# When heads leave PSUM, and what scores and the output projection wait for, in the last two layers of a two-block transformer kernel

## Chip, cores and metric

One core of a Trainium2 chip runs the whole program. The metric is the time of one execution on the device in microseconds (us), lower is better. All matrix products are in float32. The engines are named as in the profile: PE is TensorE (PEld its weight loads), DVE is VectorE, ACT is ScalarE, POOL is GpSimd, SP is the queue that issues most DMAs.

## What is computed

The input is x, 256 tokens of 1024 channels. A first block (convolution mixer, mixture of 16 experts, attention and long convolution, experts again) runs up to about 1560 us. The change doesn't touch it. A second block of two layers follows:

```python
for l in range(DEPTH):                                     # 2 layers
    x = x + 0.5 * swiglu(rms_norm(x, ffn1_norm[l]), ...)   # D_FF = 2816
    h = rms_norm(x, mix_norm[l])
    z = h @ w_in[l]
    qa, ka, va, qs, ks, vs, zg = split(z)
    qa, ka = rms_norm per head (8 heads of 64)             # neighbourhood attention
    qs, ks = rms_norm per head (8 query, 2 key heads)      # sliding window attention
    o_na = softmax(qa @ ka.T / 8 + bias_na) @ va
    o_sw = softmax_with_sink(qs @ ks.T / 8 + bias_sw) @ vs
    g = sigmoid(zg + b_gate[l])                            # 2 x 1024 gates per token
    merged = g[0] * (o_na @ w_branch_na[l]) + g[1] * (o_sw @ w_branch_sw[l])
    x = x + merged @ w_out[l]
    x = x + 0.5 * swiglu(rms_norm(x, ffn2_norm[l]), ...)
```

## The kernel before

**Layout.** Channels lie on the 128 partitions and tokens on the free axis, so a 1024-channel tensor is 8 blocks (KB = 8) of 128 x 256. Weights come through one stream of 1 MB chunks into a ring of 12 slots, in the order in which PE uses them. SP issues each chunk when PE has freed the slot that it goes to (L672). A chunk of w_in holds 256 output columns: the projection of one chunk (`project`, L1317) is two halves of 8 matmuls into one PSUM bank, 32 matmul records of 256 columns in the trace, since a float32 matmul leaves two records.

**Order of work.** Each engine has a hand-written program. Every engine has one counter, each of its instructions that matter raises it, and the others wait for a value of it. A wait for a value that the same engine has already waited for or passed is left out (`Engine.wait_ge`, L195), so a wait is emitted only where it asks for something later than all waits before it on that counter. DVE's counter follows its program order: waiting for a late DVE instruction covers all earlier ones.

**Heads** (PE L1379 to L1420, ACT L1863 to L1874, DVE L2469 to L2507). The seven groups of heads come in the order qa 0, qa 1, ka 0, ka 1, qs 0, qs 1 (two blocks each, 512 columns) and ks 0 (256 columns). They alternate between PSUM banks 5 and 4. For group i:

- PE projects it, and after that makes the sums of squares of group i-1 (`norm_heads` of PE, L1371: one matmul of 512 columns into bank 6). That matmul waits for ACT's square of group i-1 (L1373) and, where a group precedes it, for ACT's root of group i-2 (L1375).
- DVE's `copy_heads` (L2469, L2480) takes it out of its bank, multiplied by the token scale.
- ACT squares the copy (L1870), waits for the sums and takes their root (L1539).
- DVE's `norm_heads` (L2482) inverts the root (L1944, a reciprocal) and scales the group (L2488).
- The loop of DVE (L2490) runs `norm_heads` of group i-1 first and `copy_heads` of group i second.

Between the heads' end and the scores stand the values: vs (32 records of 128 columns), va of the first 128 tokens, the sums of ks, va of the last 128 tokens (L1405 to L1420). DVE takes them out, then copies the two halves of ks crosswise into KSX (L2506, L2507, the signal `ks_swapped`). KSX is read only by sliding-window scores.

**Attention** (PE L1433 to L1501). Eight pairs of heads: m = 0 to 3 are neighbourhood pairs, 4 to 7 sliding-window pairs. For each pair PE makes `scores(m)` into banks 0 and 1, projections of gates as filling, transposes of the probabilities (`turned`) and `values`. Before its scores PE waits for `ks_swapped` (L1441), and from the second pair on for DVE to have read the scores of the pair before.

**Branches and output** (PE L1477 to L1518, DVE L2549 to L2562). Eight calls of `branch(p, n)`, p = 0 to 3 and n = 0, 1, fill bank 2(p mod 2) + n with 16 records each. DVE multiplies each by its gates (`gated`, L2555) and adds the two of one p into two blocks of `merged` (L2557). Then the output projection: four chunks c into banks 0 to 3, each two halves of 8 matmuls over k, where matmul k reads block k of `merged`. PE waits for the last `merged` ahead of all of them (L1510).

Of the kernel before, what the change touches and what calls it, by code (L numbers as in the profile page):

```python
# [14 lines left out]
KB = D // P  # L15
# [528 lines left out]
def head_of(M, what, c):  # L544

    y = M.late
    return y.KS if what == "ks" else flat({"qa": y.QA, "ka": y.KA, "qs": y.QS}[what][:, 2 * c:2 * c + 2, :])


def wide(x, n):  # L550

    return x.rearrange("p (o t) -> p o t", o=1).broadcast_to([P, n, x.shape[1]])
# [141 lines left out]
def tensor_program(nc, M, S, ring):  # L694
    pe = Engine(nc.tensor)
    done, V, A, I = S.tensor, S.vector, S.scalar, S.into
# [4 lines left out]
    def mm(o, lhsT, rhs, start, stop):  # L701
        return nc.tensor.matmul(o, lhsT, rhs, start=start, stop=stop, skip_group_check=True)  # L702
# [611 lines left out]
    def layer(l):  # L1314
# [48 lines left out]

        ffn(1, y.sq8)
        mixer_2(l, project)
        ffn(2, y.sq8_heads)

    def mixer_2(l, project):
# [64 lines left out]
        def heads_of(m):  # L1433

            kind, blk = divmod(m, NA_H // 2)
            return kind, blk, [(h, DH * (h % 2)) for h in (2 * blk, 2 * blk + 1)]

        def scores(m):

            kind, blk, heads = heads_of(m)  # L1440
            pe.wait_ge(*V.at(("ks_swapped", l)))  # L1441
            if m:
                pe.wait_ge(*V.at(("biased", l, m - 1, 1)))
            for t in range(TT):
                for b, (h, p0) in enumerate(heads):
                    q = (y.QS if kind else y.QA)[p0:p0 + DH, blk, P * t:P * t + P]
                    if kind:
                        k = (y.KS if (h // 4) == h % 2 else y.KSX)[p0:p0 + DH, :]
                    else:
                        k = y.KA[p0:p0 + DH, blk, :]  # L1450
                    ins = mm(bank[b][:, T * t:T * t + T], q, k, True, True)
            ins.then_inc(*done.up(("scores_2", l, m)))
# [24 lines left out]
        def branch(p, n):  # L1477
            c, off = divmod(p, 2)
            b = 2 * (p % 2) + n
            name = ("branch", l, ("na", "sw")[n], c)  # L1480
            pe.wait_ge(*ring.landed(name))
            pe.wait_ge(*A.at(("out_2", l, NA_H // 2 * (n + 1) - 1)))
            if p >= 2:
                pe.wait_ge(*V.at(("gated", l, p - 2, n)))
            for half in range(2):
                for k in range(4):
                    ins = mm(bank[b][:, T * half:T * half + T], ring.tile(name)[:, k, 256 * off + P * half:256 * off + P * half + P],
                             y.OUT2[:, 4 * n + k, :], k == 0, k == 3)
            last = (p, n) == (KB // 2 - 1, 1)
            ins.then_inc(*(ring.free(name, 4) if last else done.up(("branch", l, p, n))))  # L1490

        pairs = NA_H
        for m in range(pairs):
            if m:
                turned(m - 1)
            scores(m)
            gates(2 * m)
            if m:
                values(m - 1)
            gates(2 * m + 1)  # L1500
# [6 lines left out]
        for p in range(2, KB // 2):  # L1507
            for n in range(2):
                branch(p, n)
        pe.wait_ge(*V.at(("merged", l, KB // 2 - 1)))  # L1510
        for c in range(KB // 2):
            name, b = ("out_2", l, c), c % 4
            pe.wait_ge(*ring.landed(name))
            for half in range(2):
                for k in range(KB):
                    ins = mm(bank[b][:, T * half:T * half + T], ring.tile(name)[:, k, P * half:P * half + P], y.merged[:, k, :],
                             k == 0, k == KB - 1)
            ins.then_inc(*ring.free(name))  # L1518
# [409 lines left out]
def vector_program(nc, M, S, ring):  # L1928
# [498 lines left out]
    def layer(l):  # L2427
# [41 lines left out]
        def copy_heads(what, c):  # L2469
            n = 1 if what == "ks" else 2  # L2470
            to, got = head_of(M, what, c), bank[HEADS_BANK[what, c]][:, 0:n * T]
            tokens = wide(y.rinv, n)
            if what in ("qa", "qs"):
                turned = lambda x: x.rearrange("p (n t q) -> p n t q", n=n, q=P)
                to, got, tokens = turned(to)[:, :, :, ::-1], turned(got), tokens.rearrange("p n (t q) -> p n t q", q=P)
            else:
                to, got = (x.rearrange("p (n t) -> p n t", n=n) for x in (to, got))
            chunk = {"qa": 0, "ka": 2, "qs": 6}
            dve.wait_ge(*(TE.at(("ks", l)) if what == "ks" else S.chunk.at(("in_2", l, chunk[what] + c))))
            v.tensor_tensor(to, got, tokens, ALU.mult).then_inc(*done.up(("head", l, what, c)))  # L2480

        def norm_heads(what, c):  # L2482
            w = T if what == "ks" else 2 * T
            i = HEADS_ORDER.index((what, c))
            inv = flat(y.var[:, 2 * i:2 * i + w // T, :])
            part = head_of(M, what, c)
            invert(("head_root", l, what, c), inv)
            v.scalar_tensor_tensor(out=part, in0=part, scalar=gain[what], in1=inv, op0=ALU.mult, op1=ALU.mult).then_inc(*done.up(("head_normed", l, what, c)))  # L2488

        for i, x in enumerate(HEADS_ORDER):  # L2490
            if i:
                norm_heads(*HEADS_ORDER[i - 1])
            copy_heads(*x)
        dve.wait_ge(*TE.at(("rinv_t", l)))
        v.tensor_copy(y.rinv_t, bank[7][:, T:2 * T].rearrange("p (t c) -> p t c", t=TT)[:, :, 0]).then_inc(*done.up())
        dve.wait_ge(*S.chunk.at(("in_2", l, 8)))
# [72 lines left out]
    for l in range(LAYERS):  # L2569
        layer(l)  # L2570
# [93 lines left out]
```

## Time and profile before

| | us |
|---|---|
| median of 3 runs | 2747.8 |
| lowest and highest run | 2745.44 and 2748.63 |
| the profiled execution's own time | 2748.07 |
| span in its trace, first to last instruction | 2746.8 |
| TensorE clock granted, mean | 0.996 of full speed |

The span leaves out 1.3 us of the execution's own time. In the trace a record's start is exact; the end of a matmul is modelled, and matmuls overlap, so distances between starts are what tells PE's pace. "Idle before" is time that the engine stood before an instruction, with what it waited for behind an arrow.

### The profile page before, as it was taken

The numbers are of one execution on the slowest core, as the hardware profiler recorded it, in microseconds if no ns is written. First come the engines' busy times: TensorE is split into PE (matmuls) and PEld (weight loads), VectorE is DVE, ScalarE is ACT, GpSimd is POOL, SyncE is SP. The second block draws the span as 40 slices with busy tenths as digits, with TensorE's granted clock in tenths as the row PEclk, the third lists the DMA queues.
The fourth block names the chain that finished last, engine by engine and source line by source line (L and its number), as shares of the span: only waits on it lengthen the run. The fifth ranks groups of instructions, "written<-read, shape, count | busy, mean of one in ns | idle before, by whom it ended". The sixth has DMA issues, their size and how long they took to land. (4 is left out here: it accounts for less than half of the span.)

```text
span 2746.8 us, 28088 instructions
## 1 busy us (share of the span) xinstructions
PE 2611.2 (95%) x12442; PEld 1745.1 (64%) x12442; DVE 753.7 (27%) x1426; ACT 378.5 (14%) x741; POOL 48.9 (2%) x33
## 2 busy tenths in 40 slices
PE   9999999889999999888799999999999999999999
PEld 4344343424468733323278887788888888778888
DVE  4961221212265411101021115521102103542110
ACT  2111110101133100000010002600001001350000
POOL 0001000000000000000000110000000100000000
PEclk9999999999999999999999999999999999999999
DMA  9652999999942699999996543234446444324430
GB/s 367 281 226 111 404 426 425 428 428 427 423 193 93 250 417 427 427 428 427 427 368 191 183 144 132 94 151 146 151 152 182 153 153 150 111 92 168 152 125 16
DMA packets 89572, 690.10 MB, mean 251 GB/s; under 512 B 25316, under 2 KB 26724, under 8 KB 28140
## 3 DMA queue, kind: packets, MB, share of 16 engines
q1 hardware_dynamic: 86960, 682.66, 62.9%
q0 software_dynamic: 848, 2.90, 0.3%
q10 hardware_dynamic: 1644, 2.76, 0.3%
q8 instruction: 98, 1.61, 0.2%
q14 instruction: 22, 0.18, 0.0%
HBM read 687.22 MB, written 1.06 MB: 251 GB/s over the span
## 5 line engine op out<-in xcount | busy, mean ns | idle before, releaser
L702 PE MATMUL bank<-normed,ring 128*128 128x256 f32 (+1 forms) x4640 | 1103.6, 398 | 5.8 <-DVE normed L2038 2.2
L702 PEld LDWEIGHTS bank<-normed,ring 128*128 128x128 f32 x4640 | 878.1, 190 | 223.3 <-issue 103.8
L702 PE MATMUL bank<-ring,moe_chosen 128*64 128x512 f32 x1504 | 334.5, 595 | 28.9 <-DMA ring<-in_stream 27.4
L702 PE MATMUL bank<-ffn_hidden,ring 128*128 128x256 f32 x1408 | 304.6, 379 | 0.0
L702 PEld LDWEIGHTS bank<-ffn_hidden,ring 128*128 128x128 f32 x1408 | 267.5, 190 | 37.1 <-issue 0.9
L702 PEld LDWEIGHTS bank<-ring,moe_chosen 128*64 128x64 f32 x1504 | 105.3, 137 | 245.9 <-issue 190.5
L702 PE MATMUL bank<-ring,moe_turned 128*64 128x512 f32 (+1 forms) x832 | 165.1, 547 | 20.1 <-DVE moe_turned L2248 18.0
L2246 DVE TENSOR_TENSOR moe_silu<-bank,moe_silu 128x512 f32<-128x512 f32 x32 | 22.1, 692 | 405.5 <-PE bank L702 405.5
L702 PEld LDWEIGHTS bank<-ring,moe_turned 128*64 128x64 f32 x832 | 54.9, 137 | 116.4 <-issue 84.6
L1855 ACT ACTIVATE gates<-gates 128x512 f32<-128x512 f32 x44 | 27.7, 629 | 523.2 <-DVE gates L2446 523.2
L2446 DVE TENSOR_TENSOR gates<-bank,late_rinv 128x512 f32<-128x512 f32 x44 | 30.4, 692 | 248.7 <-PE bank L702 248.6
L2252 DVE COPY moe_results<-bank 32x512 f32<-32x512 f32 x45 | 31.0, 689 | 221.8 <-PE bank L702 221.3
L2056 DVE SCALAR_TENSOR_TENSOR ab_z<-ab_pad_b,vectors,ab_z 128x512 f32<-128x512 f32 x120 | 90.2, 752 | 4.3
L2455 DVE SCALAR_TENSOR_TENSOR hidden<-bank,hidden 128x512 f32<-128x512 f32 x16 | 11.1, 692 | 288.1 <-PE bank L702 288.1
L1734 ACT COPY moe_results<-bank 32x512 f32<-32x512 f32 x45 | 25.8, 574 | 443.4 <-PE bank L702 443.1
L2451 DVE TENSOR_TENSOR ffn_hidden<-bank,gates 128x512 f32<-128x512 f32 x44 | 30.5, 692 | 201.1 <-PE bank L702 201.1
L702 PE MATMUL bank<-ring,normed 128*128 128x256 f32 (+1 forms) x320 | 65.8, 366 | 0.5 <-DVE cd_rinv L2299 0.5
L702 PEld LDWEIGHTS bank<-ring,normed 128*128 128x128 f32 x320 | 57.2, 198 | 8.2 <-issue 1.0
L702 PE MATMUL bank<-hidden,ring 128*128 128x256 f32 x256 | 55.8, 380 | 3.0 <-DVE hidden L2557 3.0
L1944 DVE RECIPROCAL gates<-gates 128x512 f32<-128x512 f32 (+1 forms) x14 | 43.7, 3125 | 53.3 <-ACT gates L1539 53.3
L702 PE MATMUL bank<-ab_y,ring 128*128 128x512 f32 x128 | 56.3, 592 | 0.0
L702 PEld LDWEIGHTS bank<-moe_hot,normed 128*128 128x128 f32 x384 | 45.2, 192 | 16.0 <-issue 10.5
(361 smaller groups left out, 1820.5 us busy)
## 6 DMA issues: line engine op xcount, KB each, us to landing
ring<-in_stream SPq DMA_DIRECT2D x138, 2048.0 KB, 24.6
ring<-in_stream SPq DMA_DIRECT2D x264, 1024.0 KB, 4.9
ring_low<-in_stream SPq DMA_DIRECT2D x10, 2048.0 KB, 36.6
ring_high<-in_stream SPq DMA_DIRECT2D x10, 2048.0 KB, 37.9
ring_far<-in_stream SPq DMA_DIRECT2D x9, 2048.0 KB, 34.6
hidden<-in_stream SPq DMA_DIRECT2D x10, 1024.0 KB, 36.4
normed<-in_stream SPq DMA_DIRECT2D x10, 1024.0 KB, 39.1
ring_filter_freq<-in_stream SPq DMA_DIRECT2D x6, 1024.0 KB, 15.1
```

Of the source, the lines that this page charges most:

```text
L702: return nc.tensor.matmul(o, lhsT, rhs, start=start, stop=stop, skip_group_check=True)
L1734: ins = nc.scalar.copy(m.YG[CAP * e:CAP * e + CAP, i, 0:512], bank[4][CAP * i:CAP * i + CAP, :])
L1855: nc.scalar.activation(y.sg[c % 2], y.sg[c % 2], ACT.Silu).then_inc(*done.up((tag, l, "silu", c)))
L1944: v.reciprocal(x, x).then_inc(*done.up(name))
L2056: ins = v.scalar_tensor_tensor(out=z_j, in0=ab.PB[:, :, k:k + T], scalar=tap("conv_b", k, j), in1=z_j, op0=ALU.mult, op1=ALU.add)
L2246: v.tensor_tensor(m.SG, bank[1][:, :], m.SG, ALU.mult).then_inc(*done.up((tag, "hidden", g, e)))
L2252: ins = v.tensor_copy(m.YG[CAP * e:CAP * e + CAP, i, 512:1024], bank[4][64 + CAP * i:64 + CAP * i + CAP, :])
L2446: v.tensor_tensor(sg, bank[c % 2][:, :].rearrange("p (n t) -> p n t", n=2), wide(y.rinv, 2), ALU.mult).then_inc(*done.up((tag, l, "scaled" ...
L2451: v.tensor_tensor(flat(hidden), bank[2 + c % 2][:, :], y.sg[c % 2], ALU.mult).then_inc(*done.up((tag, l, "hidden", c)))
L2455: v.scalar_tensor_tensor(out=h0[:, 2 * p:2 * p + 2, :], in0=bank[4 + p][:, :].rearrange("p (n t) -> p n t", n=2), scalar=0.5, in1=h0[:, 2 ...
```

## The change

Three edits, each applied once in each of the two layers.

- DVE's loop over the groups of heads takes group i out of its bank first and normalizes group i-1 after it. The first group and the last `norm_heads` are where they were.
- `scores(m)` waits for `ks_swapped` only for sliding-window pairs; neighbourhood pairs wait for the normalization of the group ka 1.
- The output projection no longer waits for the last `merged` at its start. It waits for DVE to have read bank 0 of `branch(2, 0)`, and each matmul k for the `merged` of its own pair of blocks, k // 2.

```diff
@@ scores(m), PE
-            pe.wait_ge(*V.at(("ks_swapped", l)))
+            pe.wait_ge(*V.at(("ks_swapped", l) if kind else ("head_normed", l, "ka", 1)))
             if m:
                 pe.wait_ge(*V.at(("biased", l, m - 1, 1)))
@@ mixer_2, PE
         for p in range(2, KB // 2):
             for n in range(2):
                 branch(p, n)
-        pe.wait_ge(*V.at(("merged", l, KB // 2 - 1)))
         for c in range(KB // 2):
             name, b = ("out_2", l, c), c % 4
             pe.wait_ge(*ring.landed(name))
+            if c == 0:
+
+                pe.wait_ge(*V.at(("gated", l, KB // 2 - 2, 0)))
             for half in range(2):
                 for k in range(KB):
+                    pe.wait_ge(*V.at(("merged", l, k // 2)))
                     ins = mm(bank[b][:, T * half:T * half + T], ring.tile(name)[:, k, P * half:P * half + P], y.merged[:, k, :],
                              k == 0, k == KB - 1)
@@ layer(l), DVE
         for i, x in enumerate(HEADS_ORDER):
+            copy_heads(*x)
             if i:
                 norm_heads(*HEADS_ORDER[i - 1])
-            copy_heads(*x)
```

## Rows read from the trace of the kernel before

**Rows 1.** The page, busy time, share of the span and instructions of each engine.
```profile
PE 2611.2 (95%) x12442; PEld 1745.1 (64%) x12442; DVE 753.7 (27%) x1426; ACT 378.5 (14%) x741; POOL 48.9 (2%) x33
```

**Rows 2.** Waits of PE from 1560 us on: total us, times, longest.
```profile
PE bank L702 <- ACT hidden L1870: 5.5, 2, 2.8
PE bank L702 <- DVE hidden L2557: 3.0, 2, 1.5
PE bank L702 <- DVE ffn_hidden L2507: 3.0, 2, 1.5
```

**Rows 3.** Waits of the SP queue from 1560 us on, same columns.
```profile
SPq L676 <- PE bank L702: 1041.9, 137, 29.4
```

**Rows 4.** Timeline of PE, layer 0, heads: start, us, instruction, idle before.
```profile
1676.49 1.02 PE L702 MATMUL bank<-hidden,kept 128*128 128x512 f32 x2
1677.35 3.62 PE L702 MATMUL bank<-normed,ring 128*128 128x256 f32 x16
1683.73 1.12 PE L702 MATMUL bank<-hidden,kept 128*128 128x512 f32 x2 [2.76 <-ACT hidden L1870]
1684.69 10.64 PE L702 MATMUL bank<-ring,normed 128*128 128x128 f32 x64
```

**Rows 5.** Timeline of DVE and ACT, layer 0, same stretch.
```profile
1677.55 0.69 ACT L1539 ACTIVATE gates<-bank,epsilons 128x512 f32<-128x512 f32 x1 [1.64 <-PE bank L702]
1678.27 3.35 DVE L1944 RECIPROCAL gates<-gates 128x512 f32<-128x512 f32 x1 [3.02 <-ACT gates L1539]
...
1682.33 0.69 DVE L2480 TENSOR_TENSOR ffn_hidden<-bank,late_rinv 128x512 f32<-128x512 f32 x1
1683.05 0.63 ACT L1870 ACTIVATE hidden<-ffn_hidden 128x512 f32<-128x512 f32 x1 [4.81 <-DVE ffn_hidden L2480]
```

**Rows 6.** Timeline of PE, layer 1: the same two steps.
```profile
2353.88 1.12 PE L702 MATMUL bank<-hidden,kept 128*128 128x512 f32 x2 [2.76 <-ACT hidden L1870]
2354.84 12.27 PE L702 MATMUL bank<-ring,normed 128*128 128x128 f32 x64
```

**Rows 7.** Windows: length, PE, PEld, DVE, ACT, POOL busy (count), PE clock, DMA share, GB/s.
```profile
1684.80:1688.20 3.40, 3.40 (x33) 3.40 (x32) 2.59 (x1) 0.69 (x1) 0.00 (x0) 1.00 0.00 0
2354.80:2358.20 3.40, 3.40 (x18) 3.36 (x17) 2.44 (x1) 0.69 (x1) 0.00 (x0) 0.52 0.02 5
...
1700.00:1780.00 80.00, 78.52 (x427) 61.86 (x427) 42.70 (x116) 51.44 (x117) 0.00 (x0) 1.00 0.33 119
```

**Rows 8.** Timeline of PE, layer 0: last values, first scores, first transposes, second scores.
```profile
1695.61 7.07 PE L702 MATMUL bank<-ring,normed 128*128 128x256 f32 x32
1704.16 1.13 PE L702 MATMUL bank<-ffn_hidden 64*128 64x256 f32 x8 [1.48 <-DVE ffn_hidden L2507]
...
1712.23 1.04 PE L705 MATMUL bank<-kept,hidden 128*128 128x128 f32 x8
1713.20 1.14 PE L702 MATMUL bank<-ffn_hidden 64*128 64x256 f32 x8
```

**Rows 9.** Timeline of DVE, layer 0, around the first scores.
```profile
1703.81 0.29 DVE L2507 COPY ffn_hidden<-ffn_hidden 64x256 f32<-64x256 f32 x1
1705.39 0.69 DVE L2518 TENSOR_TENSOR hidden<-bank,na_bias 128x512 f32<-128x512 f32 x1 [1.29 <-issue]
...
1709.49 0.62 DVE L2536 TENSOR_SCALAR hidden<-hidden,small 128x256 f32<-128x256 f32 x2
```

**Rows 10.** Timeline of PE, layer 0: projection of qa 0 with its waits, sums after it.
```profile
1630.54 7.07 PE L702 MATMUL bank<-normed,ring 128*128 128x256 f32 x32
1637.44 1.03 PE L702 MATMUL bank<-hidden,kept 128*128 128x256 f32 x4
```

**Rows 11.** Timeline, layer 0: last seven branches, last merge, start of the output projection.
```profile
1789.44 24.44 PE L702 MATMUL bank<-normed,ring 128*128 128x256 f32 x112
...
1814.64 0.69 DVE L2557 TENSOR_TENSOR hidden<-ffn_hidden 128x512 f32<-128x512 f32 x1
1815.39 6.96 PE L702 MATMUL bank<-hidden,ring 128*128 128x256 f32 x31 [1.51 <-DVE hidden L2557]
```

## The prediction

> **What bounds the kernel.** I read the page first: PE is busy for 95% of the span, DVE for 27%, ACT for 14% [rows 1], so a change pays only by what it takes out of PE's own line of work. Next the waits of PE in the last two layers, from 1560 us on: only three kinds are left, each twice, once per layer [rows 2]. PE waits 2.8 us for ACT's square of a group of heads (L1870), 1.5 us for DVE's crosswise copy of ks (L2507), 1.5 us for DVE's last merge (L2557); 11.5 us in all. The three edits touch just these. No wait for a DMA is among them. SP, for its part, waited 137 times for PE, 1041.9 us in total, to free slots [rows 3]: the weight stream follows PE, so PE running earlier finds its weights there, and SP issues them earlier by the same amount. No edit moves a DMA or a POOL instruction past anything.
>
> The page's idle times end at a modelled matmul end, so I take distances between starts instead. The pace: 32 records of 256 columns take 1637.44 - 1630.54 = 6.90 us, 0.216 us each [rows 10]. The sums of one group of 512 columns take 1677.35 - 1676.49 = 0.86 us when nothing is late [rows 4].
>
> **Edit 1, heads leave their bank first.** In the trace the ks projection starts at 1677.35 with 16 records, so PE reaches the sums of qs 1 at 1677.35 + 16 x 0.216 = 1680.81. It starts them at 1683.73, and the next work at 1684.69, that is 0.96 later, not 0.86 [rows 4]. Lost: 1684.69 - (1680.81 + 0.86) = 3.02 us. Why: qs 1 was in its bank at about 1676.5, but DVE first waited for the root of qs 0 (ACT, 1677.55 to 1678.24), ran its reciprocal (1678.27, 3.35 us) and its scaling, and copied qs 1 at 1682.33 only; ACT squared it at 1683.05 [rows 5]. The other groups hide this delay under 32 records (6.90 us); ks has only 16.
>
> With the copy first, DVE takes qs 1 at about 1676.7, done 1677.4. ACT is at the sums of qs 0 until 1678.24 [rows 5] and then squares qs 1, 0.63 us: 1678.9. PE comes at 1680.8, so 1.9 us is left. The other condition of these sums, the root of qs 0, is that same 1678.24. The reciprocal of qs 0 still starts at 1678.27, since the root sets it: the copy (0.69 us) lies in DVE's idle 3.02 us before it. Both orders run the same seven copies, reciprocals and scalings, so nothing is added. **Who is queued behind the moved wait:** normalizing group i-1 now stands behind the copy of i, which needs the projection of i ended. It cost nothing, because PE makes the sums of i-1 after that same projection. The last copy, ks, follows the scaling of qs 0, at about 1682.4 to 1682.8. Its reader on PE is the second part of va and ACT's square for the sums of ks, and PE asks for these only after vs and the first part of va, over 10 us behind the sums of qs 1 [rows 4]. So what is late next is nothing on PE. Gain 3.02 us; in layer 1 the same 2.76 us of idle stand [rows 6], so 6.0 us for both. Bounds: if the square comes late in part, down to 0; above, the 3.02 itself.
>
> **The clock behind that wait.** In layer 1 the 64 records after the wait took 12.27 us, in layer 0 10.64 us [rows 4, 6]. The granted clock was 0.52 from 2354.8 to 2358.2, the lower of its two levels (1.2 of 2.4 GHz), and 1.00 in the same place of layer 0, each after the same idle time [rows 7]. It cost 12.27 - 10.64 = 1.63 us. Without the wait there is no such hole in front, and I count the 1.63 us as gained against this profiled execution. Bounds: 0 (it comes somewhere else in an execution) and 3.3 (executions in which both layers pay it).
>
> **Edit 2, scores wait for their own keys.** The last values start at 1695.61 and take 32 x 0.216 = 6.91 us, to 1702.52; the scores start at 1704.16 [rows 8]. A switch into scores is not free: eight transposes of 128 columns, 0.108 us each (half of 0.216 for half the columns), run from 1712.23 to 1713.09, the next scores start at 1713.20 [rows 8], so 0.1 us. Lost: 1.54 us. The wait that takes its place, ka 1 normalized, lies far behind on DVE: PE has already waited for the copy of ks (ahead of the second part of va), and DVE counts this later, so no wait is emitted at all. What is late next? DVE must still make its two ks copies, which end at 1704.10 [rows 9], and the scores end at about 1702.62 + 1.23 = 1703.85 in this frame, so the first softmax starts at 1704.14 instead of 1705.39, earlier by 1.25 and not by 1.54. Its probabilities were ready at 1709.49 + 0.62 = 1710.11 [rows 9] and would be at 1708.9; PE comes for them at 1712.23 - 1.54 = 1710.7. 1.8 us of cover are left: the gain holds. 1.54 x 2 = 3.1 us. Bounds: 0.9 per layer (were the 0.29 us that DVE falls behind and another 0.3 of switching to show) and 1.64 (no switch).
>
> **Edit 3, the output projection.** Seven branches start at 1789.44; 112 records at 0.216 to 0.217 end at 1813.7, and the output starts at 1815.39 [rows 11]. Lost: 1.7 us. Now PE asks at 1813.7 for bank 0, which DVE had left by about 1804 (two branches before the last merge but one), and for merged 0 to 2, done by 1808.5. Merged 3 is needed by k = 6, after 12 records: 1813.7 + 2.6 = 1816.3; DVE has it at 1814.64 + 0.69 = 1815.33 [rows 11]. 1 us of cover. Gain 1.7 x 2 = 3.4 us.
>
> What is added: the waits inside the stream. The wait for bank 0 covers merged 0 and 1, so only k = 4 and k = 6 of the first half emit one, plus that at the start. The nearest row is the projection of qa 0: there six of the first eight matmuls wait for their own gained block, and 32 records took 6.90 us, no more than the ordinary pace [rows 10]. I take zero. Bounds: 0 and, were each to expose one weight load of about 0.2 us, 0.4 us per layer. The Trainium skill (TensorE: Matmul & The Clock Gate, the section on engine queue depths) says that PE's queue may load weights ahead of matmuls in flight; if a wait stopped that, the sum would be 0.8 us smaller. The row with six waits speaks for zero.
>
> **Sum.** 6.0 + 3.1 + 3.4 = 12.5 us, with the clock's 1.6 us 14.1 us. The profiled execution took 2748.07 us, 0.27 above the median: 2748.07 - 14.1 = 2734.0. I give this for the median too.
>
> **Rivals.**
>
> - **The clock's part is no gain.** The low stretch is luck of an execution; the median run had none, or another comes elsewhere. For it: layer 0 had the same wait and paid nothing [rows 7]. Then 2747.8 - 12.5 = 2735.3. Chance 0.25.
> - **A wait takes the place of one removed.** The nearest is the square of qs 1 with 1.9 us of cover; then merged 3, 1 us; then the first probabilities, 1.8 us. If edit 1 gave nothing, because ACT's root still held the sums back, the rest is 3.1 + 3.4 = 6.5: 2741.3, chance 0.03. If edit 2 or 3 gave nothing in either layer, or each half: 2738 to 2739, chance 0.07. Against all: the covers above.
> - **The change doesn't do what it says.** A wait left out by the counter could leave PE behind an older, later one, say if another wait just ahead already asked for the last merge. None does: PE's last DVE wait in the branches is for a gated block of p = 1. Chance under 0.01, time 2747.8.
> - **Slower: the clock falls in attention.** Attention has eight pairs per layer, and in 80 us of it PE stands for 80 - 78.5 = 1.5 us in short holes, at clock 1.00 [rows 7]. If starting it 4.6 us earlier let the clock fall there once per pair, 16 x 1.63 = 26 us would be paid, net 26 - 12.5 = 13.6 slower: 2761. It decides from the eighth such fall (8 x 1.63 = 13 us against 12.5). Against: the holes are the same before and after, both layers pass at 1.00, and the change only removes idle time. The Trainium skill (TensorE: Matmul & The Clock Gate, "A second HAM failure mode") describes a kernel whose short idles between groups made the clock go up and down; by the trace this attention doesn't. Chance 0.02.
>
> **From these to numbers.** Forecast as summed 0.62, the clock's part missing 0.25, lesser gains 0.10, no effect or slower 0.03. About 0.2% (5.5 us) is what a measurement of this kernel can tell from no change; the three runs of before spread over 3.2 us. Faster by more than that: everything except the last 0.03 and part of the case at 2741: 0.95. Within it 0.03, slower 0.02. The range: 2734.0 less the other layer's clock stretch (1.6) and half the spread of runs gives 2731; above, 2735.3 with 0.8 for waits in the stream, 1.2 for edit 2 at its lower bound and 1.2 for the runs gives 2738.5.
>
> **What would show it.** PE's waits in the last two layers are empty of L1870, L2507 and L2557. The sums of qs 1 start 3.46 us after the ks projection; the next work 0.86 behind them. DVE's copy (L2480) of each group comes before the reciprocal (L1944), about 0.2 us behind the projection's end, and the reciprocals keep their places against PE. Scores start 7.0 us after the last part of va. The output projection follows the last branch at the ordinary pace, with the merge (L2557) beside its first records. From the start of layer 0's heads to the end, everything is shifted by 3.0, then 4.6, 6.3, 9.3, 10.8 and 12.5 us. I would be wrong if PE showed new idle time at k = 4 or 6, before the first transposes, or at the sums of ks, or if the clock fell in a place where it now doesn't.

## The result and the profile after

The changed kernel takes 2732.88 us (median of 4 runs, 2731.64 to 2733.16), the kernel before 2748.22 us in the same comparison (4 runs, 2745.44 to 2750.48). The ratio is 0.9942 with a 95% interval of 0.9926 to 0.9957: faster by 0.43 to 0.74%, 15.3 us between the medians. The forecast was 2734.0 us in a range of 2731.0 to 2738.5, against 2747.8.

The profiled execution took 2733.02 us, its span is 2731.7 us. The three waits of [rows 2] are gone: from 1560 us on, the view of PE's waits has no line. The page of the changed kernel gives the engines' busy times; PE's is 3.2 us less than in [rows 1], half of which is a stretch at low clock that is gone (see below); most of the gain is idle time:

```profile
PE 2608.0 (95%) x12442; PEld 1743.8 (64%) x12442; DVE 754.1 (28%) x1426; ACT 377.6 (14%) x741; POOL 48.9 (2%) x33
```

**Edit 1.** The timeline of the changed kernel, layer 0, answers to [rows 4, 5] (start, length, instruction, idle time before it and what ended that). DVE's lines have moved down by three in the code.

```profile
1675.78 1.02 PE L702 MATMUL bank<-hidden,kept 128*128 128x512 f32 x2
...
1675.98 0.69 DVE L2483 TENSOR_TENSOR ffn_hidden<-bank,late_rinv 128x512 f32<-128x512 f32 x1 [2.05 <-PE bank L702]
...
1676.64 3.62 PE L702 MATMUL bank<-normed,ring 128*128 128x256 f32 x16
...
1676.84 0.69 ACT L1542 ACTIVATE gates<-bank,epsilons 128x512 f32<-128x512 f32 x1 [6.56 <-PE bank L702]
1677.42 0.62 ACT L1873 ACTIVATE hidden<-ffn_hidden 128x512 f32<-128x512 f32 x1
1677.56 3.35 DVE L1947 RECIPROCAL gates<-gates 128x512 f32<-128x512 f32 x1 [0.89 <-ACT gates L1542]
...
1680.09 1.02 PE L702 MATMUL bank<-hidden,kept 128*128 128x512 f32 x2
...
1680.95 10.64 PE L702 MATMUL bank<-ring,normed 128*128 128x128 f32 x64
```

DVE takes qs 1 out of its bank at 1675.98, 0.2 us behind the end of its projection, and 1.6 us ahead of the reciprocal of qs 0, which it used to follow. ACT squares it at 1677.42, behind the root, and is done at 1678.04, 2.05 us before PE asks. The sums start 3.45 us after the ks projection, and the next work 0.86 us after the sums. The reciprocal starts 0.92 us after the ks projection's start, as in [rows 4, 5].

**Edit 2.** The same timeline around the first scores, PE and DVE; it answers to [rows 8, 9].

```profile
1691.86 7.07 PE L702 MATMUL bank<-ring,normed 128*128 128x256 f32 x32
...
1698.86 1.13 PE L702 MATMUL bank<-ffn_hidden 64*128 64x256 f32 x8
1698.97 0.75 DVE L2507 TENSOR_SCALAR ffn_hidden<-bank,small 128x512 f32<-128x512 f32 x1 [3.46 <-PE bank L702]
...
1700.07 0.29 DVE L2510 COPY ffn_hidden<-ffn_hidden 64x256 f32<-64x256 f32 x1
1700.39 0.69 DVE L2521 TENSOR_TENSOR hidden<-bank,na_bias 128x512 f32<-128x512 f32 x1
...
1704.48 0.62 DVE L2539 TENSOR_SCALAR hidden<-hidden,small 128x256 f32<-128x256 f32 x2
...
1706.93 1.04 PE L705 MATMUL bank<-kept,hidden 128*128 128x128 f32 x8
```

The scores start 7.00 us after the last values start (8.55 before), while DVE still has its ks copies to make. PE comes to the transposes without waiting. A window over attention in the changed kernel (columns as in [rows 7]), with the same bounds as the last of [rows 7]:

```profile
1700.00:1780.00 80.00, 80.00 (x434) 63.48 (x435) 43.84 (x122) 55.00 (x125) 0.00 (x0) 1.00 0.33 120
```

PE's idle 1.5 us in that window of before was the single wait for `ks_swapped` at 1704.16 [rows 8], and it is gone.

**Edit 3.** The start of the output projection, timeline of layer 0, answers to [rows 11]:

```profile
1784.14 24.44 PE L702 MATMUL bank<-normed,ring 128*128 128x256 f32 x112
...
1808.42 9.88 PE L702 MATMUL bank<-hidden,ring 128*128 128x256 f32 x45
1808.62 0.69 DVE L2558 TENSOR_TENSOR ffn_hidden<-bank,gates 128x512 f32<-128x512 f32 x1 [2.76 <-PE bank L702]
1809.35 0.69 DVE L2560 TENSOR_TENSOR hidden<-ffn_hidden 128x512 f32<-128x512 f32 x1
```

The projection starts 24.28 us after the seven branches start (25.95 before) and runs on without a gap, the last merge lying beside its first records.

**The clock.** The row of 64 records behind the sums of qs 1 holds 32 of vs with 128 columns and 32 of va with 256, which the view merges. In layer 1 they took 10.64 us, as in layer 0, where [rows 6] had 12.27. Windows of the changed kernel over that stretch (columns as in [rows 7]):

```profile
1680.90:1684.30 3.40, 3.40 (x32) 3.35 (x31) 3.37 (x4) 1.10 (x2) 0.00 (x0) 1.00 0.00 0
2350.20:2353.60 3.40, 3.40 (x18) 2.99 (x17) 0.46 (x2) 0.00 (x0) 0.00 (x0) 1.00 0.65 272
```

**A finer measure than the medians.** From the start of the projection of qa 0 in layer 0 to the end of the span it is 2746.8 - 1630.54 = 1116.26 us before and 2731.7 - 1629.82 = 1101.88 us after, 14.38 less. I call this the late stretch. The rest, 0.7 us, lies in the first block, whose code is the same: over the 13 profiles of this study the late stretch starts anywhere between 1627.7 and 1632.7 us. That scatter is in every median, while the late stretch of kernels without a hole repeats to 0.1 us (below). I call a hole a stretch in which PE stands although its next work could have started. Part of the scatter is again the clock: in the first block the granted clock was 0.50 in stretches that add up to between 13.7 and 27.3 us, and the two earliest starts, 1627.7 us in e_covers and 1628.0 in e_sums_late, go with 13.7 and 17.1 us of them. It isn't all: the latest start, 1632.7 in e_after_again, has 23.9.

### The profile page after: what moved, and what is told of

Read it like the earlier page. It is cut to its first block, busy times and chain, and to the rows that moved or that the text cites. A ratio compares the mean times of both kernels' runs of the same rounds, so it can differ in the third digit from the quotient of the medians.

```text
span 2731.7 us, 28090 instructions
## 1 busy us (share of the span) xinstructions
PE 2608.0 (95%) x12442; PEld 1743.8 (64%) x12442; DVE 754.1 (28%) x1426; ACT 377.6 (14%) x741; POOL 48.9 (2%) x33
## 4 chain that ended last, share of the span: by engine, by line
PE 80%; DMA 11%; DVE 3%; issue 0%; ACT 0%; DVEq 0%
PE bank L702 79%; DMA ring<-in_stream 7%; DMA ring_high<-in_stream 3%; DMA ring_low<-in_stream 2%; PE bank L705 1%; DVE ab_z L2059 1%; DVE moe_turned L2251 0%; DVE moe_silu L2249 0%; DVE moe_results L2255 0%; DVE moe_top L2165 0%; DVE moe_max L2163 0%; DVE moe_cum L2170 0%; DVE hidden L2006 0%; ACT L1686 0%; ACT cd_product_t L1814 0%
## 5 line engine op out<-in xcount | busy, mean ns | idle before, releaser
L702 PEld LDWEIGHTS bank<-moe_hot,normed 128*128 128x128 f32 x384 | 45.2, 191 | 16.2 <-issue 10.5
L702 PEld LDWEIGHTS bank<-hidden,ring 128*128 128x128 f32 x256 | 48.6, 190 | 6.6
## 6 DMA issues: line engine op xcount, KB each, us to landing
ring_filter_freq<-in_stream SPq DMA_DIRECT2D x6, 1024.0 KB, 14.7
```

## The experiments

The table gives the late stretch, what the low clock adds to it (by how much the sums of qs 1 and the 64 records behind them exceed 0.96 and 10.64 us), and the rest. The spans are given to 0.1 us, so a late stretch is good to 0.05 us and a difference of two to 0.1. Each ratio is to the kernel before as measured beside that kernel, with medians from 2747.9 to 2750.0 us.

| kernel | median us | ratio to before, 95% | late stretch | clock's part | without it |
|---|---|---|---|---|---|
| before | 2748.2 | | 1116.26 | 1.63 | 1114.63 |
| changed | 2732.9 | 0.9942 [0.9926, 0.9957] | 1101.88 | 0 | 1101.88 |
| e_heads | 2740.6 | 0.9966 [0.9955, 0.9978] | 1108.53 | 0 | 1108.53 |
| e_scores | 2745.7 | 0.9985 [0.9976, 0.9994] | 1112.91 | 1.43 | 1111.48 |
| e_out | 2744.8 | 0.9983 [0.9974, 0.9991] | 1112.58 | 1.48 | 1111.10 |
| e_scores_out | 2741.9 | 0.9973 [0.9964, 0.9983] | 1111.20 | 3.30 | 1107.90 |
| e_after_again | 2734.1 | 0.9947 [0.9934, 0.9959] | 1101.91 | 0 | 1101.91 |
| e_one_copy | 2733.1 | 0.9944 [0.9931, 0.9958] | 1101.87 | 0 | 1101.87 |
| e_sums_late | 2732.4 | 0.9943 [0.9928, 0.9959] | 1101.90 | 0 | 1101.90 |
| e_many_waits | 2733.3 | 0.9947 [0.9933, 0.9960] | 1101.84 | 0 | 1101.84 |
| e_long_wait | 2737.7 | 0.9961 [0.9948, 0.9973] | 1105.84 | 0 | 1105.84 |
| e_covers | 2742.1 | 0.9973 [0.9964, 0.9982] | 1112.18 | see there | |
| e_hole | 2750.2 | 1.0005 [0.9995, 1.0014] | 1117.55 | 4.97 | 1112.58 |

**Each edit alone.** `e_heads` holds only the hunk of DVE's loop, `e_scores` only that of `scores`, `e_out` only that of the output projection, `e_scores_out` the last two together:

```diff
# e_heads
+            copy_heads(*x)
             if i:
                 norm_heads(*HEADS_ORDER[i - 1])
-            copy_heads(*x)
# e_scores
-            pe.wait_ge(*V.at(("ks_swapped", l)))
+            pe.wait_ge(*V.at(("ks_swapped", l) if kind else ("head_normed", l, "ka", 1)))
# e_out
-        pe.wait_ge(*V.at(("merged", l, KB // 2 - 1)))
...
+            if c == 0:
+                pe.wait_ge(*V.at(("gated", l, KB // 2 - 2, 0)))
...
+                    pe.wait_ge(*V.at(("merged", l, k // 2)))
```

> Edit 1 alone. Theory (three separate stalls of PE, each its own): 3.02 us less per layer, 6.0 us less in all, and the two waits of 1.5 us for the copies of ks and the last merge stay in each layer. If the low clock behind the sums of qs 1 goes with the wait: up to 1.6 us more. So 2740.5 to 2742.2 against 2748.2. Rival (the edits need each other, time saved in the heads is lost again at the scores): no difference, 2748.

> Edit 2 alone. Theory: the distance from the last values to the first scores falls from 8.55 to 7.0 us in each layer, 3.1 us in all: 2745.1. The waits of 2.8 us at the sums of qs 1 and of 1.5 us at the output stay. Rival (DVE still has its ks copies to make, so PE waits at the first transposes instead): no difference, with idle time in front of L705.

> Edit 3 alone. Theory: the distance from the start of the last seven branches to the output projection falls from 25.95 to 24.28 us, 1.67 us per layer, 3.3 us in all: 2744.9. Rival (waits inside the accumulation cost as much as the one that went): idle time at the fifth and seventh matmul, less than 1 us gained in all.

> The change without edit 1: 6.4 us less than before, 2741.8, if the stalls are independent. The waits of 2.8 us at the sums of qs 1 remain in both layers. The clock theory (a low stretch follows such a wait in some executions and places only) expects windows behind these sums at 0.5 in none, one or both layers; if it is tied to layer 1's place it is there again at 0.52 and in layer 0 at 1.00.

Without the clock's part: edit 1 alone 1114.63 - 1108.53 = 6.10 us, edit 2 alone 3.15, edit 3 alone 3.53. Their sum is 12.78, all three together give 1114.63 - 1101.88 = 12.75, edits 2 and 3 together 6.73 against 3.15 + 3.53 = 6.68. The three stalls are independent, and the rivals (lost again downstream, waiting at the first transposes, waiting inside the accumulation) fall. In edit 3's 3.53 us are 2 x 1.67 us by which the projection starts sooner and 2 x 0.10 us by which its first twelve records run closer (2.59 us, where they took 2.69 behind the wait). The waits of PE in the late layers of e_heads are the two that it leaves:

```profile
PE bank L702 <- DVE hidden L2557: 3.0, 2, 1.5
PE bank L702 <- DVE ffn_hidden L2507: 3.0, 2, 1.5
```

The medians say the same more coarsely. Against 2749.5 us for the kernel before beside them, e_heads gains 8.9, e_scores 3.8, e_out 4.7 and e_scores_out 7.6 us. In e_heads that is 2.8 more than 6.1, of which the clock explains about 2.0 (below); the three kernels that keep the hole also gain 0.7 to 1.1 us more by medians than by the late stretch without the clock, so medians don't settle the last microsecond. Behind the hole at the sums of qs 1 the low stretch came in layer 1 in e_scores, in layer 0 in e_out and in both in e_scores_out. Windows of e_out, layer 0 and layer 1:

```profile
1683.00:1686.00 3.00, 2.48 (x5) 1.45 (x6) 0.00 (x0) 0.84 (x2) 0.00 (x0) 0.53 0.00 0
2353.00:2356.00 3.00, 2.62 (x17) 2.15 (x18) 0.74 (x1) 1.01 (x2) 0.00 (x0) 1.00 0.02 5
```

The same of e_scores:

```profile
1683.00:1686.00 3.00, 2.02 (x12) 1.54 (x13) 0.40 (x2) 1.32 (x2) 0.00 (x0) 1.00 0.00 0
2352.00:2355.00 3.00, 2.42 (x5) 1.39 (x6) 0.00 (x0) 0.83 (x2) 0.00 (x0) 0.52 0.03 5
```

The same of e_scores_out:

```profile
1684.00:1687.50 3.50, 3.10 (x9) 2.07 (x10) 0.46 (x1) 1.03 (x2) 0.00 (x0) 0.59 0.00 0
2352.00:2357.00 5.00, 4.12 (x16) 3.45 (x17) 2.16 (x2) 1.32 (x2) 0.00 (x0) 0.66 0.01 3
```

So it is not tied to layer 1's place: it belongs to the hole and comes behind some of them. The seven profiles without a hole there (changed, e_heads, e_after_again, e_one_copy, e_sums_late, e_many_waits, e_covers) pass the place fourteen times, always at 1.00.

**The changed kernel again.**

> The changed kernel unaltered, on the chip of this batch. By the clock theory (part of the gain is that the low stretches behind the two sums of qs 1 are gone), its runs lie closer together than those of before, whose last two layers hold none, one or two such stretches of 1.6 us or so, and no window behind 1600 us is under 1.00. 2732 to 2735 against 2748 to 2750. The rival (such stretches move elsewhere in the last layers) expects one in them.

2734.11 us (5 runs, 2733.19 to 2735.91) against 2749.95 (15 runs, 2745.76 to 2751.29). The late stretch is the same to 0.03 us, and no window in it is under 1.00. The runs do lie closer, over 2.7 us against 5.5, though there are fewer of them.

**Which copies matter.** `e_one_copy` is the changed kernel with this loop:

```diff
-            copy_heads(*x)
+            if x == ("qs", 1):
+                copy_heads(*x)
             if i:
                 norm_heads(*HEADS_ORDER[i - 1])
+            if x != ("qs", 1):
+                copy_heads(*x)
```

> The changed kernel, but of the moved copies only that of qs 1 goes ahead of the norm of the group before; the other five are back in the old order. Theory (only the group ahead of the half-length ks projection was late, the others hide behind 32 records): same time as the changed kernel within 1 us, no idle time at the sums of qs 1. Rival (the gain comes from all copies together): idle time at some sums, over 1 us slower.

Late stretch 1101.87, no wait at any sums. The whole of edit 1's 6.1 us is one of the six copies that it moves: that of the group whose follower has a half-length projection.

**PE's place in line instead of DVE's order.** `e_sums_late` keeps DVE's loop of before and edits 2 and 3:

```diff
         project(name, b, None, 1).then_inc(*done.up(("ks", l)))
-        norm_heads(*before, 512)
         for t in range(TT):
             for k in range(KB):
                 ins = mm(bank[3][:, P * t:P * t + P], U[:, 0, k, P * t:P * t + P], tile[:, k, P:2 * P], k == 0, k == KB - 1)
         ins.then_inc(*ring.free(name))
+        norm_heads(*before, 512)
```

> Edits 2 and 3 kept, DVE's loop as before, but PE makes the sums of qs 1 after vs (32 records of 128 columns, 3.5 us) instead of ahead of it. Theory (it is PE's place in line that counts, not DVE's order): the 2.8 us are hidden, same time as the changed kernel within 1 us; the square of ks is then ready some 0.9 us before PE asks for it. Rival (DVE's order itself gains the time): idle time of 1 us or more at the sums of qs 1 or of ks.

Late stretch 1101.90, the same as the changed kernel, with the copy of qs 1 still late. Its timeline of PE, DVE and ACT in layer 0:

```profile
1678.27 3.73 PE L702 MATMUL bank<-ring,normed 128*128 128x128 f32 x32
...
1679.80 0.68 DVE L2483 TENSOR_TENSOR ffn_hidden<-bank,late_rinv 128x512 f32<-128x512 f32 x1
1680.51 0.63 ACT L1873 ACTIVATE hidden<-ffn_hidden 128x512 f32<-128x512 f32 x1 [4.81 <-DVE ffn_hidden L2483]
...
1681.84 1.02 PE L702 MATMUL bank<-hidden,kept 128*128 128x512 f32 x2
```

The square ends at 1681.14, 0.7 us before PE comes for it behind vs. Nothing about DVE's order is worth time by itself; what counts is that PE has other work until the square is there. Both ways reach the same end.

**The covers.** The cover of a result is the time by which it is ready before PE asks for it. `e_covers` and `e_long_wait` load DVE with reciprocals whose result nobody reads: e_covers one at each of three places, e_long_wait two at the first place only (`range(2)`).

```diff
+            if x == ("qs", 1):
+                for _ in range(1):
+                    dve.wait_ge(*done.now())
+                    v.reciprocal(flat(y.GATES[:, 14:16, :]), head_of(M, "qs", 0)).then_inc(*done.up())
             copy_heads(*x)
...
+            if m == 0:
+                v.reciprocal(flat(y.GATES[:, 14:16, :]), head_of(M, "qs", 0)).then_inc(*done.up())
...
+            if p == KB // 2 - 1:
+                v.reciprocal(flat(y.GATES[:, 14:16, :]), flat(y.t1[0])).then_inc(*done.up())
```

> The changed kernel with one idle-work reciprocal of 3.35 us on DVE at three places in each layer: ahead of the copy of qs 1, ahead of the first softmax, and ahead of the last merge. It measures the covers that the prediction gave. Theory: PE waits for what is left of 3.38 us beyond each cover: 3.38 - 1.9 = 1.5 us at the sums of qs 1, 3.38 - 1.8 = 1.6 us at the first transposes, 3.38 - 0.9 = 2.5 us at the seventh matmul of the output, 5.6 us per layer, 11 us in all slower than the changed kernel (more if the clock falls behind one). Rival (the covers are not what they seem, PE was held by something else as well): the full 3.4 us or nothing at one of the three.

> The changed kernel with two idle-work reciprocals of 3.35 us on DVE ahead of the copy of qs 1. Theory: PE waits 2 x 3.38 - 1.9 = 4.9 us at the sums of qs 1 in each layer, 9.7 us in all; and after a hole of this length the clock is low in both layers, in all or nearly all runs, for another 1.5 to 3 us each: 2733 + 9.7 + 3 to 6 = 2746 to 2749. Rival (the low stretches have nothing to do with the hole): 2742.7 and the clock at 1.00 behind it.

Both expectations missed at the copy, for the same reason: my reciprocals waited for nothing, so they began in DVE's idle 2.05 us before the projection ended. The timeline of PE in layer 0 of e_covers, at the first transposes:

```profile
1705.01 0.66 PE L705 MATMUL bank<-kept,hidden 128*128 128x128 f32 x4
1706.26 0.66 PE L705 MATMUL bank<-kept,hidden 128*128 128x128 f32 x4 [0.60 <-DVE hidden L2545]
```

The same at the start of the output projection:

```profile
1807.37 2.75 PE L702 MATMUL bank<-hidden,ring 128*128 128x256 f32 x12
1812.25 9.94 PE L702 MATMUL bank<-hidden,ring 128*128 128x256 f32 x37 [2.13 <-DVE hidden L2568]
```

At the copy PE didn't wait. At the transposes it lost 0.2 us before the first four and 1.25 - 0.43 = 0.8 us before the second four, 1.0 in all, where I expected 1.6. At the output, after exactly the twelve records that the prediction counted, it lost 1812.25 - (1807.37 + 12 x 0.216) = 2.3 us, where I expected 2.5. These are 3.3 us per layer; the late stretch grew by 10.30, so 3.7 us are left over, and the clock was low behind the holes of 2.3 us in both layers (0.66 and 0.67): in each, the 32 records behind the hole took 8.70 us where the changed kernel takes 6.91, 3.6 us in all. That the total comes near the 11 us that I expected is luck: the clock's part stands where the wait at the copy is missing. The windows behind them, e_covers:

```profile
1812.20:1815.60 3.40, 3.35 (x10) 2.81 (x11) 0.00 (x0) 0.00 (x0) 0.00 (x0) 0.66 1.01 429
2481.10:2484.50 3.40, 3.33 (x10) 2.73 (x11) 0.01 (x1) 0.00 (x0) 0.00 (x0) 0.67 1.00 424
```

e_long_wait took 2737.7 us, where 2746 to 2749 was expected and 2742.7 by the rival: the hole was shorter than either had it. The copy came 4.64 us late and PE 1.87. The timeline of DVE in its layer 0:

```profile
1675.10 6.74 DVE L2497 RECIPROCAL gates<-ffn_hidden 128x512 f32<-128x512 f32 x2
1681.76 0.63 DVE L2483 TENSOR_TENSOR ffn_hidden<-bank,late_rinv 128x512 f32<-128x512 f32 x1
```

The timeline of PE at the same place:

```profile
1677.78 3.62 PE L702 MATMUL bank<-normed,ring 128*128 128x256 f32 x16
1683.11 1.12 PE L702 MATMUL bank<-hidden,kept 128*128 128x512 f32 x2 [1.71 <-ACT hidden L1873]
```

The sums would have been due at 1677.78 + 3.46 = 1681.24. The cover of the copy is thus 4.64 - 1.87 = 2.8 us, not 1.9: the first 0.7 us of a delay vanish behind ACT's root of qs 0, which holds the square back anyway. Behind this hole of 1.9 us the clock stayed at 1.00 in both layers, so the run says nothing of the clock behind a hole of 4.9 us, which it was made for; e_hole (below) does.

**What a fulfilled wait costs.** `e_many_waits` puts a wait for a value long reached ahead of each matmul of the projections that have no wait of their own inside:

```diff
                     if first:
                         pe.wait_ge(*V.at((first, l, "gained", k)))
+                    if not first:
+                        pe.eng.wait_ge(*V.at(("moe1", "out", NE // EG - 1, KB - 1, 0)))
                     ins = mm(bank[b][:, T * half:T * half + T], tile[:, k, P * half:P * half + P], U[:, 0, k, :], k == 0, k == KB - 1)
```

> The changed kernel with 712 more waits on PE, all for a value long reached, one ahead of each matmul of the up projections and of ks in the last layers. Theory (a wait that is already fulfilled costs PE nothing in the stream): same time as the changed kernel within 1 us, 32 records still in 6.9 us. Rival (each such wait exposes a weight load, about 0.2 us): 140 us slower; any cost between divides by 712 into the price of one.

The late stretch is 1101.84, the same as the changed kernel's 1101.88 within the 0.05 us to which each is known: no cost that can be measured. The program had 720 such waits, not 712 (16 in the ks projections of the two layers, not 8). One reservation: the trace lists no waits as such, so that every one of them was carried out isn't shown.

**A longer hole.** `e_hole` is e_long_wait with three reciprocals in place of two.

> The changed kernel with three idle-work reciprocals on DVE ahead of the copy of qs 1. With two, PE waited 1.9 us from start to start and the clock stayed at 1.00. The third adds 3.38: a hole of 5.2 us in each layer, 10.5 us in all, 2744 on its own. Clock theory: behind so long a hole the clock is low in both layers in every run, 1.6 to 3.3 us more each: 2747 to 2750. Rival (the low stretch behind the sums of qs 1 in the kernel before is not caused by the hole): 2744, clock 1.00 behind both.

The time is that of the kernel before (2750.24 us, ratio 1.0005). The timeline of PE in layer 0 and in layer 1:

```profile
1686.38 2.08 PE L702 MATMUL bank<-hidden,kept 128*128 128x512 f32 x2 [5.11 <-ACT hidden L1873]
1688.25 11.97 PE L702 MATMUL bank<-ring,normed 128*128 128x128 f32 x64
...
2357.78 2.08 PE L702 MATMUL bank<-hidden,kept 128*128 128x512 f32 x2 [5.10 <-ACT hidden L1873]
2359.65 12.46 PE L702 MATMUL bank<-ring,normed 128*128 128x128 f32 x64
```

Windows over the two sums of qs 1 in e_hole, for the clock:

```profile
1686.40:1688.40 2.00, 2.00 (x3) 0.97 (x4) 2.00 (x1) 0.00 (x0) 0.00 (x0) 0.50 0.00 0
2357.80:2359.80 2.00, 2.00 (x3) 0.97 (x4) 2.00 (x1) 0.00 (x0) 0.00 (x0) 0.50 0.03 8
```

The sums took 1.87 us and the next 64 records 11.97 and 12.46 us, that is 2.24 and 2.73 us more than at full clock. Taking these 4.97 us off, the holes cost 1112.58 - 1101.88 = 10.70 us, where 10.5 was expected; the other 0.2 us are the sums, which take 0.96 us behind a hole and 0.86 without one. The rival, a low stretch that has nothing to do with the hole, falls.

## Why the prediction held

- **What bounds the kernel: right.** The time of the late layers is PE's line of work and the holes in it; three holes per layer were 12.75 of the 14.38 us, the low clock behind one of them the rest.
- **Edit 1, 6.0 us: measured 6.10.** Its place was right too, and sharper than I put it: only one of the moved copies does anything. The cover of the copy was given as 1.9 us (the square, against PE's coming); against a delay of the copy it is 2.8. The step that mis-sized it took the square to start as soon as the copy is done, though it had itself put the square behind the root.
- **Edit 2, 3.1 us: measured 3.15.** DVE's first softmax starts 8.53 us behind the last values' start (9.78 before), 1.25 earlier, as worked out. The cover at the first transposes was given as 1.8 us; it is about 2.3. I set the second head's probabilities against PE's coming for the first; PE comes for the second 0.43 us later.
- **Edit 3, 3.4 us: measured 3.53.** The sum counted the 0.10 us that the first work behind a wait takes longer at edit 1 but not here. The cover at k = 6 was 1 us in the text; the delayed merge makes it 3.38 - 2.3 = 1.1. The waits in the stream cost nothing, as the row with six waits had said: the first 12 records take 2.59 us, 0.216 each, with them.
- **The clock, 1.6 us: right for the profiled pair, a little low for medians, and in part luck.** That execution had one low stretch, 1.63 us, and it went. In the four profiles of kernels with the hole at the sums of qs 1 (2.9 us from start to start) it followed 5 of 8 holes, on average 1.57 us each (7.84 us over five). The expected share of a run is then 2 x 5/8 x 1.57 = 2.0 us. The same reasoning would have counted nothing or 3.3 us, had the profiled execution had none or two. Before to after should be 14.7 us. The medians show 15.3 in the first comparison, 15.8 in e_after_again, and 16.9, 17.6 and 14.7 in e_one_copy, e_sums_late and e_many_waits, whose late stretch is the same. What is beyond 14.7 lies within the scatter of the first block as far as is known; no run separates it.
- **The rival by which the clock's part is no gain** was right that the stretch is luck of an execution, and wrong in what follows from it. The hole brings it, as e_hole and the fourteen passages without a hole show. A median alone would hardly tell: the rival had 2735.3 us, and the five medians of kernels without a hole lie between 2732.4 and 2734.1.
- **The slower rival fell, and its ground was a misreading.** In attention the clock stayed at 1.00 in all 13 profiles. The 80 - 78.5 = 1.5 us that the prediction took for short holes spread over 80 us of attention were the one wait for `ks_swapped`, which edit 2 takes out. In the same window the changed kernel has PE busy for 80.00 us (edit 2, above). So by this view there were no short holes that a shifted start could have moved.

## What to carry to other kernels

Where one engine is busy 95% of the time, read its few remaining waits and follow each back: here the late party was a copy of 0.7 us queued behind a reciprocal of 3.35 us whose result nobody was in a hurry for, and it hurt only where PE's work between was half as long as elsewhere. Give each wait the oldest value that suffices, and put it ahead of the instruction that needs it, inside a long accumulation if need be. And price a hole of a few microseconds in PE's work above its length: behind it PE may run at half clock for a while, which added 5/8 x 1.57 = 1.0 us on average to a hole of 2.9 us here.

## What was not expected of the hardware

The low clock behind holes in PE's work, by the profiles of this study, with the holes measured from start to start: behind 12 holes of 1.5 to 1.7 us (at the scores and at the output projection) it never came, nor behind 2 of 1.9 us; it came behind 2 of 2 holes of 2.3 us, 5 of 8 of 2.9 us, and 2 of 2 of 5.3 us. The holes of 2.3 us lie at another place, the output projection, so the counts don't compare lengths alone. The granted clock was then at the lower of its two levels, 1.2 of 2.4 GHz (0.50 in the windows of e_hole). Each time it cost 1.4 to 1.8 us, and 2.2 to 2.7 us behind the longest holes. The two cheapest, 1.43 us in e_scores and 1.48 in e_out, are those of the holes of 2.9 us in which the clock fell 0.48 and 0.35 us before PE started again, so that a part of the low stretch lay in the hole.

So a hole of the same length at the same place has a price that differs from layer to layer and from profile to profile. That it also differs between executions of one kernel, and makes part of their scatter, is argued and not shown, since a kernel with the hole has one profile each. The clock of whole runs fits it: the slowest and the fastest run of e_scores, 2748.80 and 2741.04 us, had mean clocks of 0.993 and 0.998. The first block has a share in that too.

The Trainium skill (TensorE: Matmul & The Clock Gate, "Why this matters for your kernels") warns of idle gaps between bursts of matmuls, after which the clock is low again; the rows agree, and show it for shorter gaps (holes of 2.3 and 2.9 us) than that table asks one to avoid.
